# Spill rounds of 32 rows instead of 64, and three tiles' sums ahead of the first norm in a two-layer decoder step

## Chip, cores and metric

One Trainium2 chip, one NeuronCore of it, all data in float32. The metric is the device time of one execution of the whole program in microseconds (us). Engine names are those of the profile: PE (matmul) and PEld (its weight load), DVE, ACT, POOL, SP; a "q" behind a name is that engine's instruction queue.

## What is computed

The reference is one inference step of a small hybrid decoder (D = 1024) for 512 prompt tokens and 8 requests of one token, 520 rows in all. There are two layers. The first mixes over time (RWKV-7), the last attends over dilated windows of a shared K/V projection that is made between them. Each layer ends in a hierarchical mixture of experts, and each sub-layer in a norm of `ALPHA * x + f(x)`. The experts matter here:

```python
pg, gi = lax.top_k(softmax(xt @ w_gc + b_gc), 1)           # one of 4 groups
pe, ei = lax.top_k(softmax(lf_of_group), 2)                # two of its 4 experts
expert_id = gi * 4 + ei                                    # 16 experts, hidden 512
y = sum over e of comb[:, e] * ((silu(xt @ w_gate[e]) * (xt @ w_up[e])) @ w_down[e])
x = layer_norm(ALPHA * x + y, ln_g, ln_b)
```

So 520 rows make 1040 pairs of a row and an expert, unevenly spread over 16 experts. Evaluated on the inputs of this case, the reference's router gives no expert of the first layer more than 87 rows; in the last layer expert 2 gets 101, and no other expert more than 93.

## The kernel before

`expert_layer` is called once a layer (first layer with `kv` set, last layer without). Each expert has 96 places (`CAP`), three units (`SUBS`) of 32 rows. A unit is what fills PE's four column groups: `gate_and_up` multiplies 32 rows of `xT` against 128-column pieces of the weights, four of them side by side. The 16 experts go by in order, their weights (6 chunks of 1 MB each an expert) stream in on SP's queue through a ring of slots, and the rows come by an indirect DMA of POOL.

Rows past an expert's 96 places are handled afterwards in **spill rounds**. How many rounds there are is computed on DVE in `complete` during the first expert: `over` (line 1780) compares each expert's count with the steps 96, 96+64, ..., line 1782 sums them, lines 1783 to 1785 make the expert's first round; the rows' places follow (lines 1786 to 1792), and line 1793 frees POOL to gather the rows of expert 2. Lines 1806 to 1811 find the expert of every possible round and leave the number of rounds in `plan["spills"]`.

After the last expert each engine reads that number into a register and runs a loop over all possible rounds, with a branch past the body for those that are not wanted:

```python
n = spills(pe)
with pe.Fori(0, SPILLS) as i:      # SPILLS = 15; lines 1849 DVE, 1954 SP, 2039 ACT, 2209 PE, 2334 POOL
    with pe.If(i < n):             # lines 1850, 1955, 2040, 2210, 2335
```

An engine's program goes on only when its loop is through, with the empty rounds too. In a round that is wanted, SP loads the round's list and its expert's weights again (lines 1960 to 1967; 6 MB into the six oldest slots), POOL gathers the rows into `v_x` (line 2339), PE turns them (line 2214), DVE copies them to `xT` (1853), PE does gate and up (2222) for two units of 32 rows, weight slot by weight slot with a drain after each, ACT and DVE gate (2043, 1857, 1859), PE turns (2229), DVE copies (1862), PE does down (2237), ACT copies out (2047) and stores four pieces (2051).

Then comes the combine. POOL waits for all stores and gathers each of five tiles twice (line 2349), once for each of a row's two experts. DVE adds both with their weights (`statistics`, line 1871).

In the first layer (`kv`) DVE also takes the norm's statistics, and PE, behind its loop, waits for the second gather of the first tile and runs five matmuls with no use (`keep_busy`, line 1329). Then it turns the normed rows (`turn_rows`, line 2251) and makes keys and values (line 2281), whose copies by ACT are line 2084 and whose turning is line 2261.

In the last layer ACT takes the moments behind its own loop (`moments`: a sum 2058, the centre 2060, the squares 2062, the root 2064), and DVE's `normalise` scales (1893, waits for the squares), inverts the root (1895) and finishes (1900). DVE's order is written out:

```python
statistics(0)
for i in range(1, TILES):
    statistics(i)
    normalise(i - 1)
normalise(TILES - 1)
```

SP stores each tile when it is finished (line 1974).

Of the kernel before, what the change touches and what calls it, by code (L numbers as in the profile page):

```python
# [25 lines left out]
TILES = 5  # L26
# [22 lines left out]
SLOT = 2048  # L49
CAP = 96  # L50
SUBS = CAP // 32
SPILL = 64
SPILLS = 15
SPILL_AT = EXPERTS * CAP
PLACES = SPILL_AT + SPILL * SPILLS + SPILL


def tile_rows(t):
# [62 lines left out]
def constants():  # L121
    c = Layout()
    i = np.arange(128)
    same = (i[:, None] // 64 == i[None, :] // 64).astype(np.float32)
    c.add("ident", np.eye(128, dtype=np.float32))
    c.add("headsum", same)
    c.add("center", np.eye(128, dtype=np.float32) - same / 64)

    q = np.arange(64)
    twice = lambda m: np.tile(m.astype(np.float32), (2, 1))  # L130
    for level in range(6):
        size = 1 << level
# [20 lines left out]
    c.add("steps", np.repeat((CAP + SPILL * np.arange(7, dtype=np.float32))[None], 128, 0))  # L153
    c.add("spillno", np.repeat(np.repeat(np.arange(SPILLS, dtype=np.float32), EXPERTS)[None], 128, 0))
    return c


# [1516 lines left out]
def expert_layer(core, own, v_x, route, ahead, rows, x, layer, stores, feed, stop, next_stop, final_rows, kv=None):  # L1674
# [23 lines left out]
    cnt = core.sb(own, "cnt", [128, 5, 16])  # L1698
    sf = core.sb(own, "sf", [128, 2, TILES])
    ef = core.sb(own, "ef", [128, SPILLS])  # L1700
    over = v_x[:, 480:592].rearrange("p (e k) -> p e k", e=16)
    ge = v_x[:, 592:592 + 16 * SPILLS].rearrange("p (w e) -> p w e", e=16)
    stats, mv = core.sb(own, "stats", [128, TILES, 2, 6]), core.sb(own, "mv", [128, TILES, 4])
    eps, eps_set = core.sb(own, "eps", [128, 1]), core.sem("eps_set")
    gain, shift = xe
# [20 lines left out]
    turned_in = (2, 7)  # L1726
# [10 lines left out]
    def vector(dve):  # L1737
# [36 lines left out]
        def complete():  # L1774
# [5 lines left out]
            step(dve.tensor_tensor(over[:, :, :], ps[4][:, 0:16].rearrange("p (e o) -> p e o", o=1).to_broadcast([128, 16, 7]),  # L1780
                                   core.c("steps").rearrange("p (o k) -> p o k", o=1).to_broadcast([128, 16, 7]), ALU.is_gt), "counted")
# [12 lines left out]
            for k, of in enumerate((route.first, route.second)):  # L1794
# [11 lines left out]
            step(dve.tensor_tensor(ge[:, :, :], core.c("spillno").rearrange("p (w e) -> p w e", e=16),  # L1806
                                   cnt[:, 2:3, :].to_broadcast([128, SPILLS, 16]), ALU.is_ge))
            step(dve.tensor_reduce(ef[:, :], ge[:, :, :], AX, ALU.add))
            step(dve.tensor_scalar(ef[:, :], ef[:, :], 15.0, None, ALU.min))
# [39 lines left out]
        with dve.Fori(0, SPILLS) as i:  # L1849
            with dve.If(i < n):  # L1850
                dve.wait_ge(v["x_turned"], i + 2)
                for h in range(2):
                    ins = dve.tensor_copy(xT[:, 4 * h:4 * h + 4, 0:SPILL], ps[5 + h][:, :].rearrange("p (q t) -> p q t", q=4)[:, :, 0:SPILL])
                    ins.then_inc(v["x_copied"], 1)
                for u in range(2):
                    dve.wait_ge(v["sigmoid"], 2 * i + u + 1)
                    dve.tensor_tensor(sg[:, u], sg[:, u], ps[u][:, 0:128], ALU.mult).then_inc(v["gated"], 1)
                    dve.wait_ge(v["gated"], 2 * i + u + 1)
                    dve.tensor_tensor(hid[:, u], sg[:, u], ps[u][:, 128:256], ALU.mult).then_inc(v["hidden"], 1)
                for u in range(2):  # L1860
                    dve.wait_ge(v["turned"], 2 * i + u + 1)
                    dve.tensor_copy(hT[:, u], ps[turned_in[u]][:, 0:128]).then_inc(v["h_copied"], 1)

        def statistics(i):
            t = order[i]
# [127 lines left out]
    def scalar(act):  # L1993
# [41 lines left out]
        act.sem_inc(v["y_copied"], 2)  # L2035
        act.sem_inc(v["stored"], 64)
        act.wait_ge(d, steps["plan"])
        n = spills(act)
        with act.Fori(0, SPILLS) as i:
            with act.If(i < n):  # L2040
                for u in range(2):
                    act.wait_ge(v["gate_up"], 2 * i + u + 1)
                    act.activation(sg[:, u], ps[u][:, 0:128], ACT.Sigmoid).then_inc(v["sigmoid"], 1)
                act.wait_ge(v["stored"], 64 * i + 64)
                for u in range(2):
                    act.wait_ge(v["down"], 2 * i + u + 1)
                    act.activation(v_y[:, u], ps[3 + u][:, 0:256], ACT.Copy).then_inc(v["y_copied"], 1)
                act.wait_ge(v["y_copied"], 2 * i + 4)
# [60 lines left out]
    def tensor(pe):  # L2109
# [99 lines left out]
        with pe.Fori(0, SPILLS) as i:  # L2209
            with pe.If(i < n):  # L2210
# [5 lines left out]
                pe.wait_ge(v["x_copied"], 2 * i + 2)  # L2216
                for j in range(4):
                    pe.wait_ge(v_landed[j], 32 * i + 32)
                    for u in range(2):
# [4 lines left out]
                        if j == 3:  # L2224
                            ins.then_inc(v["gate_up"], 1)
                    pe.drain().then_inc(v["slot_free"], 1)
                for u in range(2):
                    pe.wait_ge(v["hidden"], 2 * i + u + 1)
                    pe.transpose(ps[turned_in[u]][:, 0:128], hid[:, u], core.c("ident")).then_inc(v["turned"], 1)
                pe.wait_ge(v["h_copied"], 2 * i + 2)  # L2230
                pe.wait_ge(v["y_copied"], 2 * i + 2)
                for j in range(2):
                    pe.wait_ge(v_landed[4 + j], 16 * i + 16)
                    for u in range(2):
                        for k in (2 * j, 2 * j + 1):
                            for r in range(4):
                                ins = pe.matmul(ps[3 + u][32 * r:32 * r + 32, 0:256], hT[:, u, 32 * k:32 * k + 32],
                                                v_ring[4 + j].rearrange("p (k n) -> p k n", k=2)[:, k % 2, 256 * r:256 * r + 256],
                                                start=k == 0, stop=k == 3)
                        if j == 1:  # L2240
                            ins.then_inc(v["down"], 1)
                    pe.drain().then_inc(v["slot_free"], 1)
        pe.wait_ge(v["y_copied"], 2 * n + 2)
        pe.sem_inc(v["begun"], 1)

        def turn_rows(i):
# [678 lines left out]
```

## Time and profile before

| | |
|---|---|
| median of 3 runs | 1710.62 us (1710.14 to 1716.27) |
| profiled execution, its own time | 1710.39 us |
| its span, first to last instruction | 1708.6 us |
| mean granted TensorE clock | 0.966 |
| PE busy | 1577.1 us (92%) |
| PEld busy | 1166.7 us (68%) |
| DVE, ACT, POOL busy | 603.0, 370.9, 193.1 us |

The span is shorter than the time by what lies around the program's first and last instruction. Times in the rows below are microseconds from the start of the span, unless marked ns. A granted clock of 1 is 2.4 GHz, 0.5 is 1.2 GHz. A group's row ends in what released the engine after its idle time. The first layer's experts end near 856 us, the last layer's near 1650.

### The profile page before, as it was taken

What the parts mean: (1) busy time and instruction counts of PE and PEld (TensorE: products, weight loads), DVE (VectorE), ACT (ScalarE), POOL (GpSimd) and SP (SyncE); (2) the same over time, 40 slices, a digit from 0 to 9 for tenths busy, and PEclk for the clock granted to TensorE, in tenths of its full rate; (3) what the DMA queues carried; (4) which work ended last, traced back from release to release, by engine and by line L of the source; (5) the groups of instructions that cost most, each with busy time, mean ns of one, the idle gap of its engine ahead of it and who ended that gap; (6) DMA issues with size and microseconds to landing.
All of it is one profiled execution on the core that took longest, in us unless ns stands there. A gap on an engine that the chain in (4) does not pass through costs nothing. (4 is left out here: it accounts for less than half of the span.)

```text
span 1708.6 us, 46813 instructions
## 1 busy us (share of the span) xinstructions
PE 1577.1 (92%) x20648; PEld 1166.7 (68%) x20648; DVE 603.0 (35%) x1713; ACT 370.9 (22%) x919; POOL 193.1 (11%) x186
## 2 busy tenths in 40 slices
PE   7999999997799999999959999999999989999980
PEld 6878867786568555555548788887878755555550
DVE  5120445665365421212154010004756532121215
ACT  1023234332510111111122000114760011111113
POOL 1000014554400010100020000000000011010002
PEclk8999999999889899999989999999999899999995
DMA  9410001000550899999991086551216389999984
GB/s 292 176 33 25 1 2 37 29 29 28 185 198 37 316 351 378 386 376 376 374 276 65 31 155 136 119 110 60 87 59 228 121 270 380 377 385 376 387 333 156
DMA packets 217976, 330.53 MB, mean 193 GB/s; under 512 B 70409, under 2 KB 117313, under 8 KB 217777
## 3 DMA queue, kind: packets, MB, share of 16 engines
q1 hardware_dynamic: 193648, 285.33, 48.9%
q0 software_dynamic: 7920, 24.78, 5.4%
q10 hardware_dynamic: 16208, 17.44, 2.9%
q8 instruction: 165, 2.70, 0.7%
q14 instruction: 35, 0.28, 0.1%
HBM read 295.14 MB, written 32.39 MB: 192 GB/s over the span
## 5 line engine op out<-in xcount | busy, mean ns | idle before, releaser
L2161 PE MATMUL bank<-ring_extra,xT 128*32 128x256 f32 x3600 | 199.7, 380 | 0.8 <-issue 0.8
L2629 PE MATMUL bank<-x_early,ring 128*128 128x256 f32 (+1 forms) x768 | 171.1, 383 | 3.1 <-PEq L198 1.6
L2161 PEld LDWEIGHTS bank<-ring_extra,xT 128*32 128x32 f32 x3600 | 115.2, 110 | 77.5 <-issue 3.7
L2629 PEld LDWEIGHTS bank<-x_early,ring 128*128 128x128 f32 x768 | 144.9, 190 | 26.1 <-issue 2.7
L2161 PE MATMUL bank<-ring,xT 128*32 128x256 f32 x2544 | 141.5, 380 | 0.8 <-issue 0.8
L1822 DVE TENSOR_TENSOR sg<-sg,bank 128x128 f32<-128x128 f32 x96 | 27.0, 281 | 273.1 <-ACT sg L2011 273.1
L2161 PEld LDWEIGHTS bank<-ring,xT 128*32 128x32 f32 x2544 | 81.6, 110 | 54.9 <-issue 3.0
L2314 POOL DMA_INDIRECT xe<-tokens,lists x30 | 27.8, 927 | 732.9 <-DVE lists L1772 360.9
L386 PE MATMUL bank<-mix,ring 128*128 128x260 f32 x448 | 100.5, 384 | 0.0
L2182 PE MATMUL bank<-ring_extra,hT 128*32 128x256 f32 x1680 | 96.6, 380 | 0.4 <-DMA ring_extra<-in_moe_w_down 0.4
L2011 ACT ACTIVATE sg<-bank 128x128 f32<-128x128 f32 x96 | 26.7, 278 | 320.3 <-PE bank L2161 320.3
L386 PEld LDWEIGHTS bank<-mix,ring 128*128 128x128 f32 x448 | 84.5, 190 | 15.3 <-ACT k L568 2.4
L2281 PE MATMUL bank<-ring_extra,x_early 128*128 128x256 f32 x384 | 84.7, 380 | 0.8 <-ACT x_early L2080 0.8
L2182 PE MATMUL bank<-ring,hT 128*32 128x256 f32 x1392 | 80.5, 380 | 2.9 <-DVE hT L1830 1.8
L2281 PEld LDWEIGHTS bank<-ring_extra,x_early 128*128 128x128 f32 x384 | 72.2, 190 | 11.0 <-issue 1.5
L2182 PEld LDWEIGHTS bank<-ring_extra,hT 128*32 128x32 f32 x1680 | 53.8, 110 | 34.9 <-issue 0.8
L2019 ACT ACTIVATE yo<-bank 128x256 f32<-128x256 f32 x96 | 36.9, 384 | 167.8 <-PE bank L2182 167.8
L1830 DVE COPY hT<-bank 128x384 f32<-128x384 f32 x32 | 17.8, 558 | 140.5 <-PE bank L2145 140.5
L2182 PEld LDWEIGHTS bank<-ring,hT 128*32 128x32 f32 x1392 | 45.2, 110 | 31.0 <-issue 3.8
L1512 PE MATMUL bank<-ring,x_early 128*128 128x256 f32 x256 | 57.6, 382 | 0.0
L1512 PE MATMUL bank<-ring,w 128*128 128x256 f32 x256 | 57.6, 382 | 0.0
L466 PE MATMUL bank<-mix,ring 128*128 128x260 f32 x256 | 57.0, 383 | 0.4 <-issue 0.4
(441 smaller groups left out, 2360.2 us busy)
## 6 DMA issues: line engine op xcount, KB each, us to landing
ring_extra<-in_moe_w_gate SPq DMA_DIRECT2D x75, 512.0 KB, 11.3
ring_extra<-in_moe_w_up SPq DMA_DIRECT2D x75, 512.0 KB, 13.1
ring_extra<-in_moe_w_down SPq DMA_DIRECT2D x37, 1024.0 KB, 15.4
ring<-in_moe_w_down SPq DMA_DIRECT2D x29, 1024.0 KB, 15.4
ring<-in_moe_w_gate SPq DMA_DIRECT2D x57, 512.0 KB, 9.8
ring<-in_moe_w_up SPq DMA_DIRECT2D x57, 512.0 KB, 13.4
ring<-in_a_w_rkv SPq DMA_DIRECT2D x12, 1024.0 KB, 6.7
expert_out<-yo ACTq DMA_DIRECT2D x128, 96.0 KB, 6.6
```

The source lines that it names most:

```text
L386: ins = pe.matmul(pair(job, h)[:, 0:HALF], w[:, kt, q * 128:(q + 1) * 128], mix[n][:, kt, half(h)], start=kt == 0, stop=kt == KT - 1)
L466: ins = pe.matmul(ps[2 * (mt % 2) + h][:, 0:HALF], w[:, kt, (mt % 2) * 128:(mt % 2 + 1) * 128], mix["v"][:, kt, half(h)], start=kt == 0, s ...
L1512: ins = pe.matmul(ps[q][:, 0:256], z[:, kt, t * 128:(t + 1) * 128], w[q][:, kt, :], start=kt == 0, stop=kt == KT - 1)
L1822: dve.tensor_tensor(sg[:, u], sg[:, u], ps[u][:, 0:128], ALU.mult).then_inc(gd, 1)
L1830: dve.tensor_copy(hT[:, :, :], ps[7][:, 0:128 * SUBS].rearrange("p (u k) -> p u k", u=SUBS)).then_inc(hc, SUBS)
L2011: act.activation(sg[:, u], ps[u][:, 0:128], ACT.Sigmoid).then_inc(sd, 1)
L2019: act.activation(yo[e % 2][:, u], ps[3 + i % 2][:, 0:256], ACT.Copy).then_inc(yc, 1)
L2161: ins = pe.matmul(ps[u][32 * q:32 * q + 32, 0:256], xT[:, kt, 32 * u:32 * u + 32], gate_up(w, kt % 2, q), start=kt == 0, stop=kt == KT - 1)
L2182: ins = pe.matmul(ps[3 + i % 2][32 * r:32 * r + 32, 0:256], hT[:, u, 32 * k:32 * k + 32], w[k // 2][:, k % 2, 256 * r:256 * r + 256], star ...
L2281: ins = pe.matmul(ps[kv_banks[f == 2][b]][:, at:at + 256], x[:, kt, f * 128:(f + 1) * 128], w[q][:, kt, :], start=kt == 0, stop=kt == KT - 1)
L2314: pool.indirect_dma_start(out=xe[e % 2][0:CAP, :], out_offset=None, in_=core.tokens, in_offset=bass.IndirectOffsetOnAxis(ap=ids, axis=0)). ...
L2629: ins = pe.matmul(ps[2 * (job % 3) + h][:, 0:n], w[:, kt_, rr, :], z[:, kt_, lo:lo + n], start=kt_ == 0, stop=kt_ == 7)
```

## The change

A spill round covers 32 places, one unit of rows, where it covered 64. To hold the same number of rows in the worst case the loops run over 28 possible rounds, where they ran over 15, and a single expert may have up to 14 rounds, where it had 7. The number of places in all stays as it was (1024 behind the experts' own). The halves `for u in range(2)` of a round's work go, on PE, DVE and ACT, and each store takes half the bytes; the round's weights are loaded as before. The comparison `over` has 16 x 14 elements for 16 x 7, `ge` 28 x 16 for 15 x 16, and the constant table is 205 columns narrower. In the last layer's combine the first tile's norm comes behind the sums of the third tile, where it came behind the second's, and so on down.

```diff
-SPILL = 64
-SPILLS = 15
+SPILL = 32
+SPILLS = 28
-PLACES = SPILL_AT + SPILL * SPILLS + SPILL
+PLACES = SPILL_AT + 1024
+ROUNDS = 14
...
-    over = v_x[:, 480:592].rearrange("p (e k) -> p e k", e=16)
-    ge = v_x[:, 592:592 + 16 * SPILLS].rearrange("p (w e) -> p w e", e=16)
+    over = v_x[:, 480:480 + 16 * ROUNDS].rearrange("p (e k) -> p e k", e=16)
+    ge = v_x[:, 480:480 + 16 * SPILLS].rearrange("p (w e) -> p w e", e=16)
...
-                for u in range(2):
-                    dve.wait_ge(v["sigmoid"], 2 * i + u + 1)
-                    dve.tensor_tensor(sg[:, u], sg[:, u], ps[u][:, 0:128], ALU.mult).then_inc(v["gated"], 1)
...
+                dve.wait_ge(v["sigmoid"], i + 1)
+                dve.tensor_tensor(sg[:, 0], sg[:, 0], ps[0][:, 0:128], ALU.mult).then_inc(v["gated"], 1)
...
-            statistics(0)
-            for i in range(1, TILES):
+            for i in range(TILES):
                 statistics(i)
-                normalise(i - 1)
+                if i >= 2:
+                    normalise(i - 2)
+            normalise(TILES - 2)
             normalise(TILES - 1)
...
-                for u in range(2):
-                    act.wait_ge(v["down"], 2 * i + u + 1)
-                    act.activation(v_y[:, u], ps[3 + u][:, 0:256], ACT.Copy).then_inc(v["y_copied"], 1)
+                act.wait_ge(v["down"], i + 1)
+                act.activation(v_y[:, 0], ps[3][:, 0:256], ACT.Copy).then_inc(v["y_copied"], 1)
...
                 for r in range(4):
-                    act.dma_start(dst[r], v_y[32 * r:32 * r + 32, :, :]).then_inc(v["stored"], 16)
+                    act.dma_start(dst[r], v_y[32 * r:32 * r + 32, 0:1, :]).then_inc(v["stored"], 16)
...
                 for j in range(4):
                     pe.wait_ge(v_landed[j], 32 * i + 32)
-                    for u in range(2):
-                        for kt in (2 * j, 2 * j + 1):
-                            for q in range(4):
-                                ins = pe.matmul(ps[u][32 * q:32 * q + 32, 0:256], xT[:, kt, 32 * u:32 * u + 32], gate_up(v_ring[j], kt % 2, q),
-                                                start=kt == 0, stop=kt == KT - 1)
...
+                    for kt in (2 * j, 2 * j + 1):
+                        for q in range(4):
+                            ins = pe.matmul(ps[0][32 * q:32 * q + 32, 0:256], xT[:, kt, 0:32], gate_up(v_ring[j], kt % 2, q),
+                                            start=kt == 0, stop=kt == KT - 1)
...
                     pe.drain().then_inc(v["slot_free"], 1)
```

The down part on PE (line 2237) and the turning of the hidden rows (2229) are halved in the same way.

## Rows read from the trace of the kernel before

**Rows 1.** The page, its first line (span of the profiled execution).

```profile
span 1708.6 us, 46813 instructions
...
```

**Rows 2.** Waits of PE, 856 to 985 us (us in total, times, longest).

```profile
...
PE bank L1329 <- DMA ring_extra<-expert_out,slots: 17.1, 1, 17.1
...
PE bank L2281 <- ACT x_early L2080: 0.8, 1, 0.8
PE bank L2261 <- ACT ring L2084: 0.7, 1, 0.7
```

**Rows 3.** Lines 2209 and 2210, first layer (min/median/max ns, first to last start).

```profile
...
L2209 PEldq ALU_OP  x15: 36/36/43, 858.1 to 868.8; - x15
...
L2210 PEldq COMPARE_BRANCH  x15: 214/221/816, 857.3 to 868.6; - x15
...
```

**Rows 4.** Timeline of all engines, first layer (start us, us, engine).

```profile
...
871.16 1.28 DVE L1871 SCALAR_TENSOR_TENSOR rows_home<-ring_extra,weights,rows_home 128x1024 f32<-128x1024 f32 x1 [21.05 <-DMA ring_extra<-expert_out,slots]
...
872.87 7.18 PE L1329 MATMUL bank<-const 128*128 128x512 f32 x10 [17.13 <-DMA ring_extra<-expert_out,slots]
...
875.92 0.20 ACT L2070 ACTIVATE mv<-mv 128x1 f32<-128x1 f32 x1 [7.34 <-DVE mv L1880]
...
879.89 1.04 PE L2251 MATMUL bank<-const,rows_home 128*128 128x128 f32 x8
...
```

**Rows 5.** The loops of DVE, ACT and POOL, first layer, columns as there.

```profile
...
L1849 DVEq ALU_OP  x15: 40/40/52, 851.4 to 858.9; - x15
...
L2039 ACTq ALU_OP  x15: 35/35/48, 861.0 to 867.2; - x15
...
L2334 POOLq ALU_OP  x15: 32/32/49, 793.2 to 799.4; - x15
...
```

**Rows 6.** Lines 1780 and 1806; then PE's waits, 1367 to 1410 us.

```profile
...
L1780 DVE TENSOR_TENSOR spill_x<-bank,const x2: 274/274/274, 592.3 to 1386.6; 128x112 f32<-128x112 f32 x2
...
L1806 DVE TENSOR_TENSOR spill_x<-const,cnt x2: 407/412/418, 598.4 to 1392.7; 128x240 f32<-128x240 f32 x2
...
PE bank L2135 <- DMA xe<-tokens,lists: 2.4, 1, 2.4
...
```

**Rows 7.** The chain that ended last, the spill round (start us, us, what).

```profile
...
1653.44 3.38 PE bank L2222 x32
...
1656.94 1.93 PE bank L2222 x32
...
1664.70 1.93 PE bank L2237 x32
...
1666.74 1.97 PE bank L2237 x32
...
```

**Rows 8.** Stretches: PE, PEld, DVE, ACT, POOL busy, clock, DMA, GB/s.

```profile
...
1656.00:1657.00 1.00, 0.88 (x16) 0.26 (x12) 0.00 (x0) 0.00 (x0) 0.00 (x0) 0.79 1.01 406
...
```

**Rows 9.** Line 1967, the down weights of the round, with the time to landing.

```profile
...
L1967 SPq DMA_DIRECT2D ring_extra<-in_moe_w_down x2: 2312/2374/2435, 1642.4 to 1645.0; - x2
...
DMA to landing us min/median/max: 16.4/17.5/18.5
```

**Rows 10.** The loops of DVE and ACT, last layer, same columns.

```profile
...
L1849 DVEq ALU_OP  x15: 40/40/40, 1664.4 to 1671.8; - x15
...
L2039 ACTq ALU_OP  x15: 35/35/35, 1671.2 to 1679.1; - x15
...
```

**Rows 11.** Timeline of all engines, last layer's combine.

```profile
...
1677.71 1.28 DVE L1871 SCALAR_TENSOR_TENSOR rows_again<-ring,weights,rows_again 128x1024 f32<-128x1024 f32 x1 [13.06 <-DMA ring<-expert_out,slots]
...
1681.17 1.06 ACT L2058 ACTIVATE ring<-rows_again 128x1024 f32<-128x1024 f32 x1 [12.05 <-DVE rows_again L1871]
...
```

**Rows 12.** Line 1900, the last step of a norm, and line 2349, the sixth gather.

```profile
...
L1900 DVE SCALAR_TENSOR_TENSOR rows_again<-rows_again,mv,xe x5: 1274/1284/1285, 1685.7 to 1704.0; 128x1024 f32<-128x1024 f32 x4, 8x1024 f32<-8x1024 f32 x1
...
L2349 POOL DMA_INDIRECT ring<-expert_out,slots x1: 1786/1786/1786, 1680.1 to 1680.1; - x1
...
DMA to landing us min/median/max: 6.3/6.3/6.3
```

More of the change, by code:

```diff
@@ L152, in constants @@
     c.add("carry", np.repeat((np.arange(EXPERTS * (TILES + 1)) % (TILES + 1) != 0).astype(np.float32)[None], 128, 0))
-    c.add("steps", np.repeat((CAP + SPILL * np.arange(7, dtype=np.float32))[None], 128, 0))
-    c.add("spillno", np.repeat(np.repeat(np.arange(SPILLS, dtype=np.float32), EXPERTS)[None], 128, 0))
+    c.add("steps", np.repeat((CAP + SPILL * np.arange(ROUNDS, dtype=np.float32))[None], 128, 0))
+    c.add("spillno", np.repeat(np.arange(SPILLS, dtype=np.float32)[None], 128, 0))
     return c
@@ L1725, in expert_layer @@
     steps = {}
-    turned_in = (2, 7)
+    turned_in = 2
     kv_banks = ((0, 1, 2), (3, 4, 7))
@@ L1779, in complete @@
             dve.wait_ge(rk, 1)
-            step(dve.tensor_tensor(over[:, :, :], ps[4][:, 0:16].rearrange("p (e o) -> p e o", o=1).to_broadcast([128, 16, 7]),
-                                   core.c("steps").rearrange("p (o k) -> p o k", o=1).to_broadcast([128, 16, 7]), ALU.is_gt), "counted")
+            step(dve.tensor_tensor(over[:, :, :], ps[4][:, 0:16].rearrange("p (e o) -> p e o", o=1).to_broadcast([128, 16, ROUNDS]),
+                                   core.c("steps").rearrange("p (o k) -> p o k", o=1).to_broadcast([128, 16, ROUNDS]), ALU.is_gt), "counted")
             step(dve.tensor_reduce(cnt[:, 1], over[:, :, :], AX, ALU.add))
@@ L1804, in complete @@
             step(dve.tensor_tensor(one(plan["weights"][:, 1, :]), one(plan["weights"][:, 0, :]), s[:, :, 7:8], ALU.mult))
-            step(dve.tensor_tensor(ge[:, :, :], core.c("spillno").rearrange("p (w e) -> p w e", e=16),
+            step(dve.tensor_tensor(ge[:, :, :], core.c("spillno").rearrange("p (w o) -> p w o", o=1).to_broadcast([128, SPILLS, 16]),
                                    cnt[:, 2:3, :].to_broadcast([128, SPILLS, 16]), ALU.is_ge))
@@ L1854, in vector @@
                     ins.then_inc(v["x_copied"], 1)
-                for u in range(2):
-                    dve.wait_ge(v["sigmoid"], 2 * i + u + 1)
-                    dve.tensor_tensor(sg[:, u], sg[:, u], ps[u][:, 0:128], ALU.mult).then_inc(v["gated"], 1)
-                    dve.wait_ge(v["gated"], 2 * i + u + 1)
-                    dve.tensor_tensor(hid[:, u], sg[:, u], ps[u][:, 128:256], ALU.mult).then_inc(v["hidden"], 1)
-                for u in range(2):
-                    dve.wait_ge(v["turned"], 2 * i + u + 1)
-                    dve.tensor_copy(hT[:, u], ps[turned_in[u]][:, 0:128]).then_inc(v["h_copied"], 1)
+                dve.wait_ge(v["sigmoid"], i + 1)
+                dve.tensor_tensor(sg[:, 0], sg[:, 0], ps[0][:, 0:128], ALU.mult).then_inc(v["gated"], 1)
+                dve.wait_ge(v["gated"], i + 1)
+                dve.tensor_tensor(hid[:, 0], sg[:, 0], ps[0][:, 128:256], ALU.mult).then_inc(v["hidden"], 1)
+                dve.wait_ge(v["turned"], i + 1)
+                dve.tensor_copy(hT[:, 0], ps[turned_in][:, 0:128]).then_inc(v["h_copied"], 1)
         def statistics(i):
@@ L2034, in scalar @@
         act.dma_start(shift[:, :], io["ln_b"][layer, 1:2, :].to_broadcast([128, D])).then_inc(got, 16)
-        act.sem_inc(v["y_copied"], 2)
+        act.sem_inc(v["y_copied"], 1)
         act.sem_inc(v["stored"], 64)
@@ L2040, in scalar @@
             with act.If(i < n):
-                for u in range(2):
-                    act.wait_ge(v["gate_up"], 2 * i + u + 1)
-                    act.activation(sg[:, u], ps[u][:, 0:128], ACT.Sigmoid).then_inc(v["sigmoid"], 1)
+                act.wait_ge(v["gate_up"], i + 1)
+                act.activation(sg[:, 0], ps[0][:, 0:128], ACT.Sigmoid).then_inc(v["sigmoid"], 1)
                 act.wait_ge(v["stored"], 64 * i + 64)
-                for u in range(2):
-                    act.wait_ge(v["down"], 2 * i + u + 1)
-                    act.activation(v_y[:, u], ps[3 + u][:, 0:256], ACT.Copy).then_inc(v["y_copied"], 1)
-                act.wait_ge(v["y_copied"], 2 * i + 4)
+                act.wait_ge(v["down"], i + 1)
+                act.activation(v_y[:, 0], ps[3][:, 0:256], ACT.Copy).then_inc(v["y_copied"], 1)
+                act.wait_ge(v["y_copied"], i + 2)
                 dst = spill_rows(SPILL_AT + SPILL * i)
                 for r in range(4):
-                    act.dma_start(dst[r], v_y[32 * r:32 * r + 32, :, :]).then_inc(v["stored"], 16)
+                    act.dma_start(dst[r], v_y[32 * r:32 * r + 32, 0:1, :]).then_inc(v["stored"], 16)
         def moments(i):
@@ L2218, in tensor @@
                     pe.wait_ge(v_landed[j], 32 * i + 32)
-                    for u in range(2):
-                        for kt in (2 * j, 2 * j + 1):
-                            for q in range(4):
-                                ins = pe.matmul(ps[u][32 * q:32 * q + 32, 0:256], xT[:, kt, 32 * u:32 * u + 32], gate_up(v_ring[j], kt % 2, q),
-                                                start=kt == 0, stop=kt == KT - 1)
-                        if j == 3:
-                            ins.then_inc(v["gate_up"], 1)
@@ L2226, in tensor @@
-                    pe.drain().then_inc(v["slot_free"], 1)
[L2227 to L2231, printed above, removed]
+                    for kt in (2 * j, 2 * j + 1):
+                        for q in range(4):
+                            ins = pe.matmul(ps[0][32 * q:32 * q + 32, 0:256], xT[:, kt, 0:32], gate_up(v_ring[j], kt % 2, q),
+                                            start=kt == 0, stop=kt == KT - 1)
@@ L2232, in tensor @@
+                    if j == 3:
+                        ins.then_inc(v["gate_up"], 1)
+                    pe.drain().then_inc(v["slot_free"], 1)
+                pe.wait_ge(v["hidden"], i + 1)
+                pe.transpose(ps[turned_in][:, 0:128], hid[:, 0], core.c("ident")).then_inc(v["turned"], 1)
+                pe.wait_ge(v["h_copied"], i + 1)
+                pe.wait_ge(v["y_copied"], i + 1)
                 for j in range(2):
                     pe.wait_ge(v_landed[4 + j], 16 * i + 16)
[L2234 to L2241, printed above, removed]
+                    for k in (2 * j, 2 * j + 1):
+                        for r in range(4):
+                            ins = pe.matmul(ps[3][32 * r:32 * r + 32, 0:256], hT[:, 0, 32 * k:32 * k + 32],
+                                            v_ring[4 + j].rearrange("p (k n) -> p k n", k=2)[:, k % 2, 256 * r:256 * r + 256],
+                                            start=k == 0, stop=k == 3)
+                    if j == 1:
+                        ins.then_inc(v["down"], 1)
@@ L2242, in tensor @@
                     pe.drain().then_inc(v["slot_free"], 1)
-        pe.wait_ge(v["y_copied"], 2 * n + 2)
+        pe.wait_ge(v["y_copied"], n + 1)
         pe.sem_inc(v["begun"], 1)
```

## Prediction

> **What bounds the kernel now.** I read the waits of PE first, then the chain of work that ended last, then the timeline at the two places that the change touches. The profiled execution took 1710.39 us, 1.8 more than its span [rows 1], and lies 0.2 under the median of the runs. PE is busy for 92% of it. The change touches little of that. What it touches are two joints, where PE has run out of experts and the next thing is late.
>
> The first joint is in the first layer. No spill round is wanted there (87 rows at most against 96 places), so all engines only run through their empty rounds. Behind its loop PE waits for a gather until 872.87, runs `keep_busy` for 7.18 us, and turns the normed rows at 879.89 [rows 4]. From there to 985 it waits for 0.8 and 0.7 us in all [rows 2]: keys and values are PE's alone, and what delays `keep_busy` delays the kernel by as much.
>
> The second joint is the last layer's end. One round is wanted (expert 2 has 101 rows, 5 too many), and the chain of work runs through it: gate and up, down, the stores, the gathers, and then DVE's sums and norms, which stand against each other without gaps from the first sum at 1677.71 to the last norm near 1705 [rows 11, 12].
>
> **The empty rounds, first layer.** This is the term that I hold to be the largest. PE's loop starts its first round at 857.1, its 15 increments lie between 858.1 and 868.8 [rows 3], so an empty round costs (868.8 - 858.1) / 14 = 0.76 us. Two taken branches of 0.22 us are most of that. Thirteen more rounds are 13 x 0.76 = 9.9 us. The loop is through at 869.0 now and at 878.9 then. Now it is hidden behind the gather by 872.87 - 869.0 = 3.8 us. Then `keep_busy` starts about 0.2 us behind the loop (a register step and two semaphore steps), at 879.15, which is 879.15 - 872.87 = 6.3 us late. The gather is no longer what it waits for, and the normed rows, ready before 879.89, aren't either. I take **+6.3**.
>
> The price hangs on whether a branch past a body half as long costs the same. The change takes from the body 49 of its 106 matmuls and transposes with their weight loads. Bounds: if PE's empty round cost what ACT's does, (867.2 - 861.0) / 14 = 0.44 us [rows 5], the loop would end at about 870, before the gather, and the term is 0. If every taken jump past the body cost what the first did, 0.816 us [rows 3] for 0.22, a round would be 1.36 us, 28 of them 38 us, the end at 895 and the term +22. The median of the jumps is 0.22, so I take 0.76. `keep_busy` ran mostly at the lower clock; when the clock rises within it may move by a microsecond or two, kept for the range.
>
> The Trainium skill, Advanced Engine Details and Errata, section Control Flow Timing, states about 108 ns for a compare-and-branch. PE's row shows twice that. By the page an empty round would be 0.22 us shorter, 28 of them would end near 872.8, and this term would be about 0 instead of 6.3; the trace disagrees, and I go by it.
>
> The other engines' loops grow too. DVE: (858.9 - 851.4) / 14 = 0.54 us, so the end moves from 859.1 to 866.0, before its first sum at 871.16. ACT: from 867.3 to 873.1, then a table load of 1.3, with its first root due at 875.92: 1.6 us of cover. POOL: 13 x 0.44 from 799.5, a long way before its gathers [rows 4, 5]. SP next acts on the first normed tile at 879 and its loop ends near 874. All hidden: 0.
>
> **The plan on DVE, both layers.** `over` has 224 elements for 112. The row with 240 elements takes 412 ns and that with 112 takes 274 [rows 6]: 1.08 ns an element, 0.12 us for the comparison and 0.12 for the reduction behind it. Both lie ahead of line 1793, which frees the gather of expert 2, and PE stands 2.4 us for that gather in the last layer [rows 6] and in the same way in the first. So 2 x 0.24 = **+0.5**. `ge` with 448 elements adds 0.2 twice, while DVE is idle over a microsecond next: 0. The constants are 128 x 205 x 4 bytes, 105 KB, less to load; PE waits for no constant at the start, so 0, at best -0.3.
>
> **The spill round, last layer.** Turning and copying 32 rows saves about 0.3 us. The first block of gate and up took 3.38 us for 32 records at the lower clock, later ones 1.93 [rows 7]; the granted clock rose within 1656 to 1657 (mean 0.79) [rows 8]. The blocks start about 0.3 us behind the end of the one before, which is the drain and stays. With half the records, from 1653.2: the first block ends and drains at 1655.2, the second at 1657.0 (it sees the clock rise at 1656.4), the third at 1658.2, and gate and up end at 1659.3, where they ended at 1663.0. The 1.7 us of sigmoid, gating, turning and copying stay, so down can start at 1661.0 for 1664.70. Its first half is through at 1662.2. Its second half needs the last chunk of weights: issued at 1645.0, 18.5 us to landing, 1663.5 [rows 9]. Now that is covered (1666.74 [rows 7]); then PE waits 1.3 us for it, and down ends at 1664.6 for 1668.7. The copy, the stores and their landing keep their lengths. So the round gives 4.1 us to the gathers, of the 5.4 that PE saves: the first gather lands at 1673.6 for 1677.7.
>
> **Who takes it.** DVE's loop: first increment at 1664.4 now, about 1660.6 then. Its 27 empty rounds at (1671.8 - 1664.4) / 14 = 0.53 [rows 10] end at 1675.1: DVE starts its sums 2.6 us earlier, not 4.1. ACT's loop starts behind the stores, at 1671.2 now, 1667.1 then. With (1679.1 - 1671.2) / 14 = 0.56 a round [rows 10] it is through at 1682.4, where it was at 1679.2, two microseconds ahead of the sums it waits for (1681.17 [rows 11]). Now ACT is late. DVE is through with three tiles' sums by about 1683.6 (the sixth gather, now landing at 1680.1 + 6.3 = 1686.4 [rows 12], then at 1682.3), and here the new order shows: it has those sums to do while ACT is still in its empty rounds. ACT's moments then take what they took: 4.5 us from its start to DVE's last step of the first norm (1681.17 to 1685.7 [rows 11, 12]), so that step starts at 1686.9. Between the first such step and the last, DVE has seven blocks of sums or norm in 18.3 us now, 2.6 each [rows 12]; then six, 15.7. The last starts at 1702.6 for 1704.0: **-1.4**.
>
> The bounds: with ACT's rounds at the first layer's 0.44, ACT would be through at 1679.3, DVE would never stand, and its 26 us of blocks from 1675.1 and 1.3 of remaining stalls give -3.3. And the new order by itself costs: moved ahead of the norm, the third tile's sums would meet the sixth gather 0.8 us early, so -1.4 falls to about 0 where the round gives less than I say. PE's and POOL's loops end near 1685 and 1656, before anyone asks.
>
> **Sum.** 1710.4 + 6.3 + 0.5 - 1.4 = **1715.8 us**, 0.3% over now. About 0.5% (8.6 us) is what a measurement of this kernel can tell from no change.
>
> **Rivals.**
> *Cheap jumps.* PE's jump gets cheaper with the shorter body, and the loop stays behind the gather. For it: DVE, ACT and POOL, with small bodies, pay 0.44 to 0.54 a round. Against: their whole instruction mix is cheaper, and PE's backward branch, not taken, still costs 86 ns. Time: 1710.4 + 0.5 - 1.4 = 1709.5, or 1707.6 with ACT at 0.44. Chance 0.14. (By the page's 108 ns the result would be this one.)
> *Jumps that fetch.* Slower by over 0.5%: PE's taken jumps cost more in the new layout, each as much as the first one of the first layer. It decides once a round averages over 0.88 us, (882.0 - 857.1) / 28, since the first layer then loses over 9.4. At 1.36 a round the time is 1710.4 + 22 + 0.5 - 1.4 = 1731. Against: of the 15 jumps of line 2210 only the first cost that; their median is 0.221 [rows 3]. Chance 0.06. The Trainium skill, Runtime: NRT & Kernel Launch, section Instruction fetch mechanics, says that a taken branch whose target lies outside the fetched window stalls for a DMA fetch; the trace shows one slow jump that fits it and none that repeats.
> *Two rounds.* If more than 32 rows spilled, the round's 6 MB would be loaded twice, some 16 us at 400 GB/s [rows 8]. With 5 rows it can't be; 0.01.
> *The round's gain arrives whole.* If DVE and ACT leave their loops in time, 4.1 less 0.8 for the order: 1713.9. It lies inside the forecast.
>
> **How the numbers follow.** Forecast 0.79, spanning 1713.9 (ACT cheap, or the round's gain whole) to 1718.7 (nothing from the round, keep_busy 1.5 us longer), and a little of it beyond. Range 1708.0 to 1719.5: it holds the forecast and most of the cheap jumps. Slower by over 0.5% (above 1719.2): 0.06 + 0.01 and 0.04 of the forecast, 0.11. Faster (under 1702.1): nothing above reaches it, 0.03. Same: 0.86.
>
> **What would show it.** PE's loop in the first layer through near 879 with 28 increments 0.76 apart, `keep_busy` starting behind it and not behind a gather, PE's turning of rows near 886. `over` near 0.39 us. One round in the last layer, PE waiting for the last down chunk, stores about 4 us earlier, DVE's first sum released by its own loop, ACT's first moment at about the end of its loop, and a last store some 1.4 us earlier within the layer. It is wrong if PE's rounds have another price, if the shift of 6.3 us is taken up in the attention that follows, or if a second round runs.

## The result and the profile after

The changed kernel took 1718.62 us, median of 7 runs (1717.11 to 1727.46), beside 1714.31 us for the kernel before (7 runs, 1708.44 to 1716.27). The ratio on record is 1.0041, 95% interval 1.0027 to 1.0055: slower by some 7 us, and clearly so. (The two medians alone would give 1.0025, the means of the seven runs each 1.0040, so the size is less sure than the sign.) The profiled executions took 1710.39 and 1717.23 us, +6.8 where the sum said +5.4.

```profile
span 1715.4 us, 47132 instructions
...
```

Waits of PE, 856 to 1040 us, answering to [rows 2]. Nothing but its own instruction queue holds `keep_busy` (line 1330 here), and the wait for the query weights, 1.5 us before, is 2.2:

```profile
...
PE bank L1330 <- issue: 23.3, 1, 23.3
PE bank L2624 <- DMA ring<-in_b_w_q: 2.2, 1, 2.2
...
```

The same wait in the kernel before (856 to 1040 us there too):

```profile
...
PE bank L2629 <- DMA ring<-in_b_w_q: 1.5, 1, 1.5
...
```

PE's loop, lines 2207 and 2208 now, answering to [rows 3]: 28 increments, (879.4 - 859.1) / 27 = 0.75 us apart, though the body is half as long. The slow first jump (0.93) stays the only one in this loop.

```profile
...
L2207 PEldq ALU_OP  x28: 36/36/43, 859.1 to 879.4; - x28
...
L2208 PEldq COMPARE_BRANCH  x28: 214/214/932, 858.1 to 879.1; - x28
...
```

Timeline of the first layer, as [rows 4]:

```profile
...
871.67 1.28 DVE L1870 SCALAR_TENSOR_TENSOR rows_home<-ring_extra,weights,rows_home 128x1024 f32<-128x1024 f32 x1 [20.77 <-DMA ring_extra<-expert_out,slots]
...
876.49 0.20 ACT L2068 ACTIVATE mv<-mv 128x1 f32<-128x1 f32 x1 [1.76 <-DVE mv L1879]
...
879.86 7.61 PE L1330 MATMUL bank<-const 128*128 128x512 f32 x10 [23.33 <-issue]
...
887.31 1.04 PE L2246 MATMUL bank<-const,rows_home 128*128 128x128 f32 x8
...
```

DVE's first sum and ACT's first root are 0.5 and 0.6 us later, no more than PE's last expert products were (0.8): both loops stayed hidden. PE alone is late, 23.3 us idle for 17.1, and turns the rows at 887.31, 7.4 later.

The wider comparison, which takes 391 ns where the narrow one took 274 [rows 6], then the gather of expert 2 in the first layer, before and after. Counted from PE's turning of expert 1's rows, the gather is issued 0.23 us later, but it lands in 8.3 us for 7.1, and PE waits 3.1 us for it instead of 1.6:

```profile
...
L1781 DVE TENSOR_TENSOR spill_x<-bank,const x2: 391/391/391, 592.2 to 1394.8; 128x224 f32<-128x224 f32 x2
...
```

```profile
...
who waited for it (us, times):
...
  PE bank L2135: 1.6, 1
...
DMA to landing us min/median/max: 7.1/7.1/7.1
```

```profile
...
who waited for it (us, times):
...
  PE bank L2133: 3.1, 1
...
DMA to landing us min/median/max: 8.3/8.3/8.3
```

The chain through the last layer's round, and granted clock (sixth column) of its stretches, answering to [rows 7, 8]:

```profile
...
1661.66 1.93 PE bank L2219 x16
...
1665.74 1.94 PE bank L2219 x16
1667.78 1.11 PE bank L2219 x16
...
1670.60 1.07 PE bank L2232 x16
1671.78 1.11 PE bank L2232 x16
...
```

```profile
...
1665.00:1667.00 2.00, 1.89 (x20) 0.61 (x16) 0.00 (x0) 0.00 (x0) 0.00 (x0) 0.50 0.67 266
1667.00:1668.00 1.00, 0.90 (x12) 0.16 (x8) 0.00 (x0) 0.00 (x0) 0.00 (x0) 0.64 0.51 205
1668.00:1669.00 1.00, 0.85 (x16) 0.27 (x8) 0.00 (x0) 0.09 (x1) 0.00 (x0) 1.00 0.51 209
...
```

The blocks of gate and up have half the records, but three of the four run at 1.2 GHz and take 1.93 us, as long as the double ones at 2.4 GHz did. The clock rises at 1667.7, 6 us into the round's products (before, 3 us in). So down begins 8.9 us behind the round's first product, for 11.3; its weights, issued at 1652.4 and landed by 18.3 us later, are there, and the wait that I expected for them isn't. In other executions it is: in the traces of e13, e17 and e14 (below), where the products were faster, PE waited 2.4, 2.0 and 0.8 us for the last weights. In e13:

```profile
...
PE bank L2232 <- DMA ring_extra<-in_moe_w_down: 2.4, 1, 2.4
...
```

The last layer's loops, the combine and the last steps of the norms, as [rows 10 to 12]:

```profile
...
L1850 DVEq ALU_OP  x28: 40/40/40, 1670.3 to 1684.6; - x28
...
L2039 ACTq ALU_OP  x28: 35/35/38, 1675.4 to 1690.6; - x28
...
```

```profile
...
1677.47 0.96 POOL L2344 DMA_INDIRECT ring<-expert_out,slots  x1 [25.11 <-DMA expert_out<-spill_y]
...
1684.87 8.24 DVE L1870 SCALAR_TENSOR_TENSOR rows_again<-ring,weights,rows_again 128x1024 f32<-128x1024 f32 x6 [14.33 <-issue]
...
1690.82 1.06 ACT L2056 ACTIVATE ring<-rows_again 128x1024 f32<-128x1024 f32 x1 [17.46 <-DVE rows_again L1870]
...
1693.58 1.28 DVE L1892 SCALAR_TENSOR_TENSOR rows_again<-rows_again,mv,xe 128x1024 f32<-128x1024 f32 x1 [0.47 <-ACT ring L2060]
...
```

```profile
...
L1899 DVE SCALAR_TENSOR_TENSOR rows_again<-rows_again,mv,xe x5: 1273/1284/1285, 1695.3 to 1710.8; 128x1024 f32<-128x1024 f32 x4, 8x1024 f32<-8x1024 f32 x1
...
```

The gathers' first issue is 4.4 us earlier, counted from the last expert's last gate product, DVE's first sum starts 3.1 us after its data had landed, because its loop isn't through, and ACT's loop ends at 1690.8. DVE has done six sums (three tiles) meanwhile and then stands 0.5 us for ACT, and 0.25 for the root. From the last gate product to DVE's end it is 66.4 us for 68.1.

### The profile page after: what moved, and what is told of

It is laid out like the page before. It is cut to its first block and busy times, and to the rows that moved or that the text cites. A ratio compares the mean times of both kernels' runs of the same rounds, so it can differ in the third digit from the quotient of the medians.

```text
span 1715.4 us, 47132 instructions
## 1 busy us (share of the span) xinstructions
PE 1573.6 (92%) x20551; PEld 1163.8 (68%) x20551; DVE 602.5 (35%) x1710; ACT 369.6 (22%) x917; POOL 192.5 (11%) x186
```

## Experiments

Times are ratios to the kernel before, run on the same chip in the same rounds (the kernel before had medians of 1717.1, 1717.3, 1711.0, 1713.4 and 1711.9 us in the five groups e1 to e4, e5 to e8, e9 to e12, e13 to e16, e17 and e18; each group ran on one chip, the first two on the same one, and the third and the last on another). Two stretches are read from each trace: PE's idle time ahead of `keep_busy`, and the time from the last expert's last gate product to DVE's last instruction ("the end"; 68.1 us before, 66.4 in the changed kernel). Each trace is of one execution, and the end isn't well repeated: a second trace of the changed kernel (e16) has 65.2.

**e1, all loops short.** Changed kernel, `with ENGINE.Fori(0, SPILLS)` to `Fori(0, 15)` on all five. It drops rounds past 15, of which there are none.

> The changed kernel with its five loops over 15 possible rounds instead of 28; rounds stay at 32 places and the new order of the norms stays. (The plan still counts up to 28 rounds; more than 15 would go undone, and one is wanted here.) Theory: the loss is 13 empty rounds on PE in the first layer, and in the last layer ACT's and DVE's empty rounds swallow part of what the shorter round gives. So keep_busy starts when the second gather lands, near 873 as before, ACT is out of its last loop before the first tile's sums, and the time is 6.2 + 0.4 for the first layer and 1.5 to 2.5 for the last below the changed kernel: about 8.5 us less, and some 1.5 to 2 under the kernel before. Rival (the loss comes from the order of the norms or from the shorter round itself): within 2 us of the changed kernel.

0.9986 (0.9971 to 1.0000). PE waits for the gather again, 16.1 us; the end is 65.7 us. Waits of PE in that stretch:

```profile
...
PE bank L1330 <- DMA ring_extra<-expert_out,slots: 16.1, 1, 16.1
...
```

**e2, PE's loop alone.** Kernel before:

```diff
-        with pe.Fori(0, SPILLS) as i:
+        with pe.Fori(0, 28) as i:
```

> The kernel before with only PE's loop over 28 possible rounds; everything else as it was, rounds of 64 places, the other four loops over 15. Theory: this alone brings the first layer's loss, keep_busy starting 6.2 to 6.5 us late and nothing else moved: 6 to 7 us more than the kernel before. An empty round costs 0.75 us with the long body as with the short one. Rival (other parts of the change made the loss): under 2 us more.

1.0037 (1.0024 to 1.0050): one number, in the kernel before, costs about as much as the whole change did:

```profile
...
PE bank L1329 <- issue: 23.2, 1, 23.2
...
```

**e9, the reverse.** Changed kernel with `pe.Fori(0, 15)`.

> The changed kernel with PE's loop alone over 15 possible rounds, the other four over 28. Theory: the first layer's loss is PE's loop and nothing else, so keep_busy starts 15.2 to 17.2 us behind the last expert's down products, as in all kernels with 15 rounds on PE or none (23.2 to 23.5 with 28), and about 7 us come back; the last layer stays as it is. A stretch of slow control steps (about 0.7 us each while POOL issues its gathers) needs several engines in their loops at once: with PE out it should be shorter or gone in the first layer. Rival (the loss comes from any engine's long loop): keep_busy stays at 23.

1.0013 (0.9999 to 1.0027); 17.4 us, held by the gather:

```profile
...
PE bank L1330 <- DMA ring_extra<-expert_out,slots: 17.4, 1, 17.4
...
```

**e11, DVE and ACT short.** Changed kernel with `dve.Fori(0, 15)` and `act.Fori(0, 15)`.

> The changed kernel with DVE's and ACT's loops over 15 possible rounds, PE, SP and POOL over 28. Theory: the last layer is then like e1's: DVE starts its sums when the first gather lands (4.2 us behind the first gather's issue, for 7.4 in the changed kernel) and ACT is in time; the first layer keeps PE's 23.2 to 23.5 us. With two of the looping engines out, no slow control steps in the last layer. Time 3 us under the changed kernel where that has no slow steps, and 14 under where it has them. Rival (slow steps come from the length of any one loop): they stay on PE.

1.0033 (1.0021 to 1.0045). DVE's first sum stands 4.4 us behind the first gather's issue, for 7.4; the end is 63.8 us, 2.6 less than in the changed kernel's first trace and 1.4 less than in e16; PE's 23.4 us stay:

```profile
...
PE bank L1330 <- issue: 23.4, 1, 23.4
...
```

**e12, SP and POOL short.** Changed kernel with `sp.Fori(0, 15)`, `pool.Fori(0, 15)`.

> The changed kernel with SP's and POOL's loops over 15 possible rounds, PE, DVE and ACT over 28. Neither SP nor POOL is waited for behind its loop, in either layer. In the first layer SP's 28 rounds ran into the gathers' issue, as one of three engines there (ACT, PE, SP). Theory: if it is the number of control steps at once that makes them slow, the first layer's slow steps go with SP out of it, and the last layer's, where SP and POOL are through before the gathers, stay: 1.006 to 1.009 on a chip where the changed kernel has 1.009. Rival (one long loop is enough): both layers as in e5.

1.0041 (1.0027 to 1.0055), the changed kernel's own ratio: these two loops cost nothing that can be told. It showed none of the slow control steps that are described under e3, so it says nothing on them.

**e3 and e6, the old order.** Changed kernel with the four lines of sums and norms put back, run twice.

> The changed kernel with the old order of sums and norms in the last layer's combine. In the changed kernel ACT came out of its loop at 1690.75 and DVE, which had three tiles' sums to do meanwhile, stood 0.5 and 0.25 us for it. Theory: with two tiles' sums only, DVE would stand for ACT from about 1690.4 to 1693.6, 2.7 us more, so the time is 2.5 to 3 us more than that of the changed kernel. Rival (the order is worth nothing, or costs the 0.8 us of the early sixth gather): from 0.8 less to 0.3 more.

> The same kernel as e3. If the stretch of slow control steps belongs to this program, it is there again, at the same place behind the gathers' first, and the time is again about 1.010 of the kernel before. If it came with that chip or that moment, the time is that of the changed kernel plus 2.5 to 3 us, 1.006.

1.0101 (1.0087 to 1.0116) and 1.0124 (1.0107 to 1.0141). **e5** is the changed kernel beside e6:

> The changed kernel as it is, run beside the next three on one chip, since e3 took 16 to 18 us more than the kernel before of its call, where 9 to 10 were expected, and its trace shows several engines spending about 0.7 us on single branch and register steps of their loops, in both layers, for a stretch of some 11 us. Theory: that stretch comes with the old order only by chance, or by the length of the loops in any kernel with 28 rounds. Then this kernel shows it in some of its executions too, and its time is 1.004 to 1.007 of the kernel before. Rival (the stretch belongs to the old order): always 1.004, no such steps in the trace.

1.0089 (1.0071 to 1.0108), so e6 is 0.35% behind e5, about 6 us. Only about half of that can be the order's own: from DVE's first sum to its end it is 30.1 us in e6 for 27.3 in e5, 2.8 more, near the 2.7 expected; another 3.0 are in the first layer, where PE stood 26.5 us for 23.5 and the order plays no part. Both had slow control steps: in e3, e5, e6 and e8, all on one chip, engines in their loops spend 0.7 us on single steps (register operations and branches) while POOL issues its gathers. Increments of ACT (line 2039) and DVE (line 1850) in e5's last layer, and its timeline: the first sum comes 14.8 us behind the first gather's issue, not 7.4.

```profile
...
L2039 ACTq ALU_OP  x28: 3/35/711, 1680.7 to 1703.3; - x28
...
L1850 DVEq ALU_OP  x28: 3/40/708, 1675.5 to 1697.2; - x28
...
```

```profile
...
1682.72 0.96 POOL L2344 DMA_INDIRECT ring<-expert_out,slots  x1 [26.86 <-DMA expert_out<-spill_y]
...
1697.48 2.69 DVE L1870 SCALAR_TENSOR_TENSOR rows_again<-ring,weights,rows_again 128x1024 f32<-128x1024 f32 x2 [21.68 <-issue]
```

**e8, ACT alone short.** Changed kernel with `act.Fori(0, 15)`.

> The changed kernel with ACT's loop alone over 15 possible rounds, the other four over 28. In the changed kernel ACT left its loop at 1690.8 and DVE had its first three tiles' sums done at 1693.1. With 13 x 0.56 = 7.3 us less ACT is there at 1683.5, before the first tile's sums (1687.5), and its squares are ready before DVE asks. DVE then stands only 0 for ACT instead of 0.47 + 0.25: theory 0.7 us less than the changed kernel, the first layer unchanged. Rival (ACT's late exit is what holds the last layer back, and the shorter round's 4 us come out without it): 2 us or more less.

1.0079 (1.0060 to 1.0098) for 1.0089 of e5. With slow steps in both, PE's stretch is 27.0 us; it doesn't decide.

**e4, no empty rounds.** Changed kernel, each engine's loop split:

```diff
-with pe.Fori(0, SPILLS) as i:
-    with pe.If(i < n):
-        ...
+with pe.If(n > 0):
+    one_round(0)
+with pe.If(n > 1):
+    with pe.Fori(1, SPILLS) as i:
+        with pe.If(i < n):
+            one_round(i)
```

> The changed kernel with the first round taken out of the loop: one branch past round 0 if no round is wanted, and one branch past the whole loop if fewer than two are, on all five engines. It handles the same 28 rounds. Theory: no empty rounds in either layer. In the first layer keep_busy starts with the gather again (6.2 us and 0.4 less). In the last layer DVE and ACT wait for the gathers, which land about 4.3 us earlier than in the kernel before, less what the third tile's sums wait for the sixth gather (0.8): 3 to 3.5 us for 1.7. Together 8 to 9 us less than the changed kernel and 1.5 to 3 under the kernel before. Rival (the program's longer code costs fetches at the branches): no better than e1, or over 1 us for each branch taken past the loop.

0.9977 (0.9963 to 0.9992). PE 16.3 us, the end 62.1. The branch past the loop isn't free on PE. It took 6.1 us in the first layer and 3.6 in the last, as the expectation's rival had it, and is hidden only because the gather lands 7.5 us after it:

```profile
...
L2258 PEldq COMPARE_BRANCH  x2: 3558/4826/6095, 862.9 to 1670.4; - x2
...
```

The other kernels with the split paid 7.2 and 3.5 (e7), 6.2 and 4.0 (e10), 4.4 and 1.3 (e14); each time it was over 5.4 to 8.3 us before `keep_busy` started. What PE does in these microseconds no run shows. The other engines' branches showed nothing of the kind. **e7** is the same split in the kernel before:

> The kernel before (64 places a round, up to 15 rounds, old order) with the first round taken out of the loop as in e4. Theory: in the first layer nothing changes (PE's loop was hidden behind the gather), in the last layer DVE's and ACT's loops were through before the gathers and the sums, so nothing either: within 1 us of the kernel before. What e4 gains on this one is then the shorter round's (3 to 3.5 us). Rival (empty rounds cost the kernel before too, by what they do to other engines and queues): over 2 us less than the kernel before.

1.0002 (0.9986 to 1.0018), the end 67.0. So empty rounds cost the kernel before nothing that can be told. With the split in both, the shorter round is worth 4.9 us at the end; by the ends of e10 and e14 (63.0 and 64.6) it would be 4.0 and 2.4.

**e10, e4 with the old order.**

> The kernel of e4 (rounds of 32 places, first round outside the loop) with the old order of sums and norms. With no empty rounds ACT is in time, so the new order has nothing to hide and costs the wait for the sixth gather. Theory: from the first sum to the last norm DVE takes 27.5 us as in the kernels with the old order whose loops were short (28.1 and 28.3 in e1 and e4), so 0.5 to 0.8 us less than e4; in time not to be told from e4: 0.996 to 0.999 of the kernel before. Rival (the new order helps without the loops too): that stretch at 28.3 or more.

0.9990 (0.9979 to 1.0002), not to be told from e4. From the first sum to DVE's end it is 27.7 us, in e4 28.3: without late loops the new order gives nothing there, and costs about the half microsecond expected.

**e13 and e15, the comparison.** e13 is the changed kernel with `ROUNDS = 7`, e15 the kernel before with 14 steps in `over` (and `ge` moved behind it).

> The changed kernel with the comparison of counts at 16 x 7 elements, as before (up to 7 rounds for one expert; one is wanted). Theory: the two instructions take 274 and 270 ns again, the gather of expert 2 is issued 0.23 us earlier and lands in about 7.1 us in the first layer; PE turns expert 2's rows 15.05 to 15.35 us behind expert 1's in the first layer (16.4 to 16.9 in the changed kernels) and 15.0 to 15.5 in the last (15.7 to 16.1). In all 1.5 to 2 us less than e16. Rival (the longer landing has another source): 16.4 stays, less 0.24.

> The kernel before with the comparison of counts at 16 x 14 elements and nothing else. Theory: the gather of expert 2 is issued 0.23 us later and lands in 8.2 to 8.8 us in the first layer, PE is 1.3 us later there and 0.5 us in the last layer: 1.5 to 2 us more in the profile, at the edge of what the times can tell. Rival: 0.5 us.

e13: 0.9999 (0.9984 to 1.0015), beside 1.0042 (1.0028 to 1.0057) for **e16**, the changed kernel in the same group; e15: 1.0008 (0.9991 to 1.0024).

> The changed kernel beside the others. Theory: 1.004 without slow control steps, 1.009 with them, by the chip. Behind the last expert's down products keep_busy starts 23.2 to 23.5 us later unless the steps are slow.

e16 showed no slow steps and 23.4 us. The traces give e13 less than its time does: PE turns expert 2's rows 15.9 us behind expert 1's in the first layer, for 16.6 in e16, with a landing of 8.0 us; 15.8 for 15.7 in the last. But e13's trace is of the slowest of its ten executions (1718.90 us, median 1713.67), so it can't explain its median. e15's landing is 6.6 us, so the 0.23 us doesn't make the gather slow by itself: that theory fell. PE still turned expert 2's rows 16.2 us behind expert 1's in e15, but so it did in e18 (16.3), which has the narrow comparison: in both the granted clock of that stretch was 0.79, and PE came to the rows after the gather had landed.

**e17 and e18, the width of the constant table alone.** `c.add("pad", np.zeros((128, 8), np.float32))` in the changed kernel and in the one before.

> The changed kernel with 8 more columns in its constant table, which nobody reads, so that what lies behind it in SBUF moves by 32 bytes (the ring starts at 24192, a multiple of 64). Theory (addresses matter, 3 us): 1.0025 of the kernel before for the changed kernel's 1.0042. Rival (the comparison's width is all of e13's gain): 1.0042.

> The kernel before with the same 8 columns (the ring starts at 25024, as in e15). Theory (addresses matter, 3 us): 0.998 of the kernel before; e15's 1.0008 then holds 4 us for the wider comparison. Rival (only the comparison matters): 1.000, and e15's 1.4 us is the comparison's price, which agrees with the traces.

1.0033 (1.0021 to 1.0045) and 1.0004 (0.9991 to 1.0017). Addresses do nothing that can be told to the kernel before, and nothing sure to the changed one.

**e14, what is won and nothing else.** The split of e4, the old order, `ROUNDS = 7` (more than 320 rows for one expert would go undone).

> Rounds of 32 places, the first round outside the loop, the old order of the norms, and the comparison at 16 x 7. Theory: it keeps only what is won, the shorter round: 3.5 to 4 us in the last layer, and loses nothing in the first, so 0.9975 to 0.9985 of the kernel before. Rival: as e10, 0.999.

0.9959 (0.9941 to 0.9976): 7 us faster than the kernel before, the best of all. PE's stretch is 14.3 us, the end 64.6. It differs from e10 by `ROUNDS` alone and is 0.31% under it (on another chip), the second pair in which the narrow comparison comes with several microseconds; how much of the 7 us is the shorter round's was not separated.

```profile
...
PE bank L1330 <- DMA ring_extra<-expert_out,slots: 14.3, 1, 14.3
...
```

## Why the prediction was right and wrong

The forecast said slower by 5.4 us, 0.3%, and called that "no change" at 0.86. The measured 0.41% lies inside the half percent too, but its interval excludes zero. The step that failed first is therefore "about 0.5% is what a measurement of this kernel can tell from no change": seven runs of each kernel told the ratio to 0.14% either way, and its lower bound is 1.0027. A sum with a sign and a price of 6 us had to give its weight to "slower". The time itself, 1718.6 us, lies inside the range.

From profile to profile, by stretches, +6.8 is:

| stretch | forecast | traces |
|---|---|---|
| PE idle ahead of `keep_busy`, first layer | +6.3 | +6.2 |
| `keep_busy`, partly at the lower clock | 0 (range) | +0.4 |
| from turning expert 1's rows to turning expert 2's, both layers (the plan on DVE) | +0.5 | +1.8 |
| last expert of the first layer | 0 | -0.6 |
| behind `keep_busy` up to the last layer's experts (the wait for query weights is 2.2 for 1.5) | 0 | +0.7 |
| last layer behind its last gate product | -1.4 | -1.7 |
| all else: ahead of the first layer's experts -1.4, its first expert +1.3, rest +0.1 | 0 | 0.0 |

- *The empty rounds, first layer.* Right, place, cause and price: 0.75 a round with the halved body, no cheap jump and none of the loop's jumps but the first one slow (both rivals fell), `keep_busy` behind the loop. Shown from both sides by e2, which puts the loss on the kernel before with one number, and by e9, which takes most of it off (1.0013 is left, not clear of 1). The cover was a little lucky in one direction: the gather let PE go after 14.3 to 17.4 us in the profiles of kernels with a short loop, and the profile before had 17.1, so over many executions the step costs 6 to 9 us, not 6.3.
- *The jump's price.* PE's jumps stayed at 214 to 221 ns; going by the row was right. The 108 ns that the Trainium skill states (Advanced Engine Details and Errata, Control Flow Timing) don't agree with PE's rows in any kernel here.
- *The plan on DVE.* The instructions were sized right (391 ns forecast as 0.39) and the gather is issued 0.23 us later. The term was mis-sized all the same, +1.8 us in the traces for +0.5: it priced the delay of the issue and took the landing as fixed. The landing went from 7.1 to 8.3 us in the first layer, and PE stood 3.1 us for it. The landing was 8.2 to 8.8 us in nine of the thirteen traces of new kernels with the wide comparison, 6.8, 6.8, 7.5 and 7.7 in the others (e4, e5, e12, e17), and 8.0 and 7.8 in the two with the narrow one (e13, e14); in all kernels with rounds of 64 it was 6.1 to 7.2. e15 (6.6) shows that the later issue alone doesn't do it, e13 (8.0) that taking it away doesn't undo it in that trace. By the times e13 is 0.43% under e16, e15 only 0.08% over the kernel before, and e18 0.04%. With intervals of 0.15% each, e13 beside e16 fits a price of 4 to 11 us and e15 one of at most 4, so the two hardly agree. What makes the gather land later in most of the new kernels, and why the times give e13 so much, stays open.
- *The spill round.* Gain of 4.4 us to the gathers for a forecast 4.1, and the nearness is in part luck, because it came by another way: not PE waiting for its last weights but PE at the lower clock for 6 us. The clock's rise came about 3 us later within the round than before. The same products took 7.2 us in the changed kernel's first trace, 6.0 in its second (e16), and 4.6 in e3, e4 and e8, where the clock didn't fall in the round. I had taken the moment of one trace as fixed. The expected wait for the last weights is real (0.8 to 2.4 us in e13, e14 and e17), but not in every execution.
- *Who takes it.* Right: DVE out of its loop 3.1 us past the first gather's landing, ACT at the very end, six sums done meanwhile. e11 gives 1.4 to 2.6 us back; e6 beside e5 shows that the new order covers 2.8 us of ACT's lateness, with slow steps in both, and e10 that it is worth nothing without.
- *The slow steps* were in no forecast. The changed kernel has 1.0041 in the result and 1.0042 in e16, but 1.0089 in e5, whose trace shows them.

## What to carry on

A loop over the worst case with a branch per turn has a price per possible turn, on every engine, wanted or not; before widening it, ask on each engine what its last turn is now hidden behind, in the layers where no turn is wanted as well. Here one number, 15 to 28, cost the kernel 6 to 7 us, more than the 4.9 that halving the work could give, and a branch past the whole loop (e4; in e14 with two more edits) turned the change into a gain. That branch has a price too, 4.4 to 7.2 us on PE in the first layer, and is hidden here only because the gather takes longer still. When a sum has a sign and its largest term a place and a mechanism, weigh the verdict by what several runs can resolve, not by a round threshold.

## Not expected of the hardware

- A taken compare-and-branch on PE's queue, back to the start of a loop or past one body, took 0.21 to 0.22 us (medians; the first of the first layer 0.6 to 1.2), on ACT, POOL and DVE 0.05 to 0.06, with the long body as with the short one; an empty round took 0.75 us on PE, 0.53 on DVE, 0.44 on POOL, and on ACT 0.44 in the first layer and 0.56 in the last.
- On one chip, in all four profiled kernels there that had four or five loops of 28 rounds (e3, e5, e6, e8), single register and branch steps took 0.7 us, on SP, ACT and PE in the first layer (in e5 not on PE) and on DVE, ACT and PE in the last, from 1.3 to 6.5 us behind the first gather's issue until at most 13.7 us behind it, and not again. Four kernels on the same chip with short loops, none, or PE's alone long (e1, e2, e4, e7) had none, nor had any kernel on two other chips. All executions here were recorded by the profiler; whether the recording of so many control steps has a part in it can't be said from these runs.
- The branch on PE past the whole loop took 4.4 to 7.2 us in the first layer and 1.3 to 4.0 in the last (e4, e7, e10, e14), for 0.21 to 0.22 past one body. The other engines' branches there stayed under 0.1 us.
